# Last head pair's Q and K weights in a third buffer, V_a weights and mask factors issued earlier

## The reference, cut to what matters

```python
h = rms_norm(x, norm_mix_pre)
u_a, v_a, q, k, v_b, g_a, g_b = split(h @ w_in)
# branch A: chunked causal gating
v = layer_norm(gelu(v_a)); y_a = gelu(u_a) * (tril(w_s) @ v + b_s)     # per chunk and group
# branch B: each head under (window, dilation) = (128,1), (512,4), (2048,16)
s = q k^T / 8 - slope * distance;  p = exp(s - max);  o = p v_b / sum(p)  # mixed by the denominators
merged = sigmoid(g_a + b0) * (y_a @ w_a_proj) + sigmoid(g_b + b1) * (y_b @ w_b_proj)
x = x + rms_norm(merged @ w_out)
x = x + rms_norm(square(relu(rms_norm(x) @ w_ff1)) @ w_ff2)
```

## Time and profile before

| | us |
|---|---|
| three runs, median (lowest to highest) | 1197.66 (1196.62 to 1198.12) |
| the profiled execution, its own time | 1197.87 |
| its span on the slowest core (core 5) | 1196.3 |
| PE busy in it | 1112.4 (93%) |
| DVE busy | 742.4 (62%) |
| ACT busy | 529.0 (44%) |
| POOL busy | 133.7 (11%) |

### The profile page before, as it was taken

One profiled execution on the slowest core, in us unless ns is written; L12 is line 12 of the kernel. 1 busy time (PEld: TensorE's weight loads), 2 busy tenths in 40 slices (PEclk: granted clock), 3 DMA queues, 4 the chain that ended last, 5 costly groups with the idle time before them and its releaser, 6 DMA issues.

```text
span 1196.3 us, 20810 instructions; the slowest of 8 cores (1191.0 to 1196.3 us)
## 1 busy us (share of the span) xinstructions
PE 1112.4 (93%) x7304; PEld 564.6 (47%) x7304; DVE 742.4 (62%) x1230; ACT 529.0 (44%) x797; POOL 133.7 (11%) x235
## 2 busy tenths in 40 slices
PE   3799999999878999999999999889999999999994
PEld 1376556655445444544444444434444444444441
DVE  5757777777757643854554556877783167773426
ACT  5537877788846764122122135563321124331120
POOL 0000000001110431000000012530000031000013
PEclk9899999999989999999999999999999999999997
DMA  9558877788713418987677879964466469548413
GB/s 234 141 134 172 148 152 136 153 146 148 116 41 56 72 18 115 115 192 213 176 183 202 224 218 277 300 212 149 154 200 222 142 189 301 177 149 272 145 71 141
DMA packets 94183, 197.55 MB, mean 165 GB/s; under 512 B 39041, under 2 KB 55553, under 8 KB 89218
## 3 DMA queue, kind: packets, MB, share of 16 engines
q1 hardware_dynamic: 83778, 150.08, 41.3%
q0 software_dynamic: 10304, 46.14, 24.2%
HBM read 194.11 MB, written 56.62 MB: 210 GB/s over the span
## 4 chain that ended last, share of the span: by engine, by line
PE 80%; DVE 5%; issue 5%; ACT 4%; DMA 4%; POOL 2%; SPq 0%; DVEq 0%; POOLq 0%; ACTq 0%
PE pst L195 79%; ACT sb_Et L629 2%; DMA sb_xt<-x 1%; DMA sb_gfin<-gains 1%; DMA sb_wva<-w_va 1%; DVE sb_hx L1180 1%; ACT sb_Lr L700 1%; PE pst L199 1%; POOL sb_st L978 1%; DVE sb_sn L1178 1%; POOL sb_st L980 0%; DVE pst L1178 0%; DVE sb_xo L992 0%; ACT sb_junk L1164 0%; DVE sb_hT L497 0%
## 5 line engine op out<-in xcount | busy, mean ns | idle before, releaser
L629 ACT ACTIVATE sb_Et<-pst 128x1024 bf16<-128x1024 f32 (+1 forms) x160 | 150.3, 973 | 43.9 <-PE pst L195 29.7
L195 PE MATMUL pst<-sb_r,sb_hid 128*128 128x512 bf16 x640 | 139.1, 379 | 0.0
L641 DVE TENSOR_TENSOR sb_PT<-sb_Et,sb_EB 128x1024 bf16<-128x1024 bf16 (+2 forms) x200 | 110.2, 569 | 39.2 <-ACT sb_Et L629 25.7
L195 PE MATMUL pst<-sb_hT,sb_wqk 128*128 128x512 bf16 x512 | 126.3, 394 | 0.9 <-DVE sb_hT L497 0.9
L195 PE MATMUL pst<-sb_merged,sb_r 128*128 128x512 bf16 x512 | 121.6, 379 | 1.2 <-DVE sb_tp L990 1.2
L926 ACT ACTIVATE sb_sg<-pst,sb_small 128x512 f32<-128x512 f32 x64 | 44.0, 687 | 172.7 <-PE pst L195 120.0
L195 PE MATMUL pst<-sb_hT,sb_wg 128*128 128x512 bf16 x512 | 116.7, 379 | 0.0
L1074 ACT ACTIVATE sb_sn<-pst 128x512 f32<-128x512 f32 x96 | 57.0, 597 | 106.3 <-PE pst L195 105.9
L195 PEld LDWEIGHTS pst<-sb_r,sb_hid 128*128 128x128 bf16 x640 | 62.6, 98 | 75.6
L195 PE MATMUL pst<-sb_TB,sb_r 128*128 128x512 bf16 x384 | 94.5, 384 | 0.3 <-DVE sb_hid L1077 0.3
L195 PEld LDWEIGHTS pst<-sb_merged,sb_r 128*128 128x128 bf16 x512 | 50.0, 98 | 61.6 <-issue 2.0
(11 more groups left out here) (117 smaller groups left out, 1605.3 us busy)
## 6 DMA issues: line engine op xcount, KB each, us to landing
w_bf<-w POOLq DMA_DIRECT2D x32, 512.0 KB, 10.0
sb_PB<-w_bf SPq DMA_DIRECT2D x32, 512.0 KB, 6.5
w_comb<-sb_PB SPq DMA_DIRECT2D x32, 512.0 KB, 5.4
sb_r<-w_comb SPq DMA_DIRECT2D x32, 512.0 KB, 4.2
sb_r<-w_comb SPq DMA_DIRECT2D x16, 1024.0 KB, 5.0
sb_r<-w_bf SPq DMA_DIRECT2D x32, 384.0 KB, 4.0
sb_r<-w_bf SPq DMA_DIRECT2D x12, 1024.0 KB, 5.0
sb_xt<-x SPq DMA_DIRECT2D x16, 512.0 KB, 12.5
```

Source lines behind the costliest of these rows:

```text
L195: e.matmul(out, lhsT=l, rhs=r, start=st, stop=sp, skip_group_check=True))
L629: P.act(lambda e: e.activation(out=et[:, :, 0:W], in_=psall[:, sb:sb + 2, 0:W], func=AF.Exp, scale=0.125), 2 * W, [], [et.key()], [sb, sb ...
L641: P.dve(lambda e: e.tensor_tensor(out=o, in0=i0, in1=i1, op=ALU.mult), n, rk, [pt.key()], rate=2, name="mask")
```

## The change

Pair 7's Q and K weights get a buffer of their own, `wqk2`, at 64 KiB, over the parts of `stgV0` for classes 0 and 1. Their load is no longer recorded with pair 5 (priority 560) but with pair 6 (570), and depends on pair 5's output passes of classes 0 and 1 instead of on `proj_qk(5)`. The four quarters of `wva` get priorities 620 to 623 instead of 720 to 723. `load_eb(hp + 1)` gets priority `b0 - 10` instead of `b0 + 50`, ahead of `load_v(hp + 1)` at `b0 + 15` or `b0 + 40`. The homes of `hTc` for tiles 0 to 6 become 68, 70, 92, 104, 160, 64, 66.

```diff
@@ -425,6 +425,7 @@
     wqk = [buf(f"wqk{i}", (144 + 4 * i) * K, [8, 256]) for i in range(2)]
+    wqk.append(buf("wqk2", 64 * K, [8, 256]))
     wvb = [buf(f"wvb{i}", (152 + 4 * i) * K, [8, 256]) for i in range(2)]
@@ -459,7 +460,7 @@
     def load_wqk(hp, prio, after=None):
-        d = hp % 2
+        d = hp % 2 if hp < NHP - 1 else 2
         P.dma("pool", lambda e: e.dma_start(out=wqk[d][:].rearrange("p k c -> p (k c)"), in_=wqk_d[hp]), 1e6, f"wqk{d}", [],
@@ -526,8 +527,9 @@
-                P.pe([(ps(bk), wqk[d][:, kc, 128 * j:128 * j + 128], hT[:, kc, 512 * w:512 * w + 512], kc == 0, kc == 7, 512, False)
-                      for kc in range(8)], [wqk[d].key(), hTw[w]], [bk])
+                wq = wqk[d if hp < NHP - 1 else 2]
+                P.pe([(ps(bk), wq[:, kc, 128 * j:128 * j + 128], hT[:, kc, 512 * w:512 * w + 512], kc == 0, kc == 7, 512, False)
+                      for kc in range(8)], [wq.key(), hTw[w]], [bk])
@@ -713,9 +715,11 @@
         if hp < NHP - 1:
-            load_eb(hp + 1, b0 + 50, anchor[0] or gate[15])
-            if hp < NHP - 2:
+            load_eb(hp + 1, b0 - 10, anchor[0] or gate[15])
+            if hp < NHP - 3:
                 load_wqk(hp + 2, b0 + 60)
+            elif hp == NHP - 2:
+                load_wqk(hp + 1, b0 - 30)
@@ -747,14 +751,14 @@
-    hTc = [buf(f"hTc{i}", o * K, [8, 128]) for i, o in enumerate((64, 66, 68, 70, 92, 104, 160, 198, 200, 202))]
+    hTc = [buf(f"hTc{i}", o * K, [8, 128]) for i, o in enumerate((68, 70, 92, 104, 160, 64, 66, 198, 200, 202))]
@@
         P.dma("pool", lambda e, q=q: e.dma_start(out=wva[:, 2 * q:2 * q + 2, :].rearrange("p k c -> p (k c)"), in_=wva_d[q]), 1e6, f"wva{q}",
-              [], [wva.key((2 * q, 2 * q + 2))], prio=M0 - 80 + q)
+              [], [wva.key((2 * q, 2 * q + 2))], prio=M0 - 180 + q)
```

## The result

The changed kernel took 1201.53 us (median of 8 runs, 1198.07 to 1205.31) against 1197.81 for the kernel before (8 runs): a ratio of 1.0032, 95% interval 1.0019 to 1.0045. It is slower, by 3.7 us. The likeliest case had +1.1 us, 1198.8, and its own range, 1196 to 1200, did not hold; the whole range, 1193 to 1203.5, did. Rival two (the load held up behind the V reload, +3.1 with the landing of one bad core) describes what happened.

A forecast was written before the change was run, and what follows sets the result against it. PE, busy 93% of the span, was taken as the bound. Its losses, 18.55 us after against 17.5 before, gave +1.1 us on 1197.87; with the median 0.2 lower, 1198.8 us; own range 1196 to 1200, whole range 1193 to 1203.5.

The forecast's parts named there:

- The likeliest case: Whole kernel: PE loses 18.55 us after against 17.5 before, +1.1 us, 1198.8 us; chance 0.41.
- Rival two: At Q/K group 0, pair 7's load is held up behind the V reload: +3.1 to +6.5 us, 1200.8 to 1204.2; chance 0.25.
- PE's order up to group 0: After pair 5's scores: two S0 jobs, output pass 2, two S0, then Q/K group 0, reached at about 305.5 us.
- The mask factors: At each pair's start, EB going ahead of the V1 reload gains nothing: zero, at most 0.5 us either way.
- Rival one: At Q/K group 0, pair 7's load lands within 7.4 us, in time: -5.8 us, 1191.9 us; chance 0.27.
- idle until PE is at group 0: From pair 5's last scores (298.0) to Q/K group 0 (305.5), PE idles 3.8 us; bounds 1.5 and 4.5.
- wait for pair 7's weights: Before Q/K group 0, PE waits 4.6 us for the late load, with a landing of 12.0 us.
- lower clock: After the wait at Q/K group 0, PE loses 2.25 us at the lower clock; bounds 0 and 3.5.
- scores of pair 6, first class: In pair 6's first classes, no idle time counted, as moved Q/K groups fill PE: 0 us.
- pair 6's end: Between pair 6's output passes 2 and 3, V_a fillers are missing: 2.9 us idle; bounds 0 and 3.9.
- pair 7 and after attention: In pair 7 and at attention's end, PE's loss stays as before: 1.88 + 3.10 = 5.0 us.
- Rival three: After pair 6's output pass 3, the stall moves to V_a tile 2: about 3 us more, 1202 us; chance 0.07.

The follow-up runs named there:

- experiment seven: Kernel before with only the mask factors' priority changed, so that EB goes ahead of the V1 reload on SP; ratio 0.9998.
- five: Changed kernel with only the two w_bf issues of pair 5's classes 0 and 1 moved to pair 6; ratio 0.9972.
- experiment three: Changed kernel with those w_bf issues moved to pair 6 and V_a quarter 0 issued after pair 7's weights have landed; ratio 0.998, 1195.6 us.
- one: Changed kernel with pair 7's Q and K weights back in wqk1, loaded with pair 5; new priorities and hTc order kept; ratio 0.9984.
- two: Kernel before with only the third home wqk2 for pair 7's Q and K weights, its later load and its use; ratio 1.005.
- nine: The changed kernel again, beside the kernel before on one chip, for the spans of all cores; ratio 1.0045.
- four: Kernel before with a second copy of V_a quarter 1 for V_a tiles 0 to 6, instead of a third weights' home; ratio 0.9976, 1195.8 us.
- eight: Kernel before with the second copy of V_a quarter 1 and pair 5's class 0 and 1 w_bf issues moved to pair 6; ratio 0.9951, 1190.5 us.
- six: Changed kernel without the V reload for pair 6, whose output passes use what pair 4 left in the buffers; ratio 0.9978.

## Why the prediction was right or wrong

*What was right.* The places. The V_a wait is gone on every core. The load takes the w_bf's place at 298 (297.87). PE's order up to group 0 came out, and the arrival there to 1 us. The mask factors are worth nothing (experiment seven). Rival one is real and has its price: where the load is in time, as in five, the median core gains 3.8 us of the 5.8 forecast. The rule of the Trainium skill's "DMA: Bandwidth & Descriptors", section "Anatomy of one DMA — SWDGE (gpsimd) path", gives 3.2 us for this transfer, an estimate. No run reached it: the nearest are the 5.0 to 5.2 us on seven cores of experiment three, with nothing ahead in the queue, and in the loaded queue it was 8.4 to 17.7.

*Where the sum failed: its terms, on core 2.* First two windows on core 2 (stretch and its us; busy us and instructions of PE, PEld, DVE, ACT and POOL; PEclk, DMA share, GB/s):

```profile
348.90:364.40 15.50, 10.90 (x150) 7.47 (x148) 10.34 (x17) 11.23 (x15) 3.08 (x3) 0.89 0.00 1
364.40:392.00 27.60, 26.86 (x325) 16.48 (x322) 19.55 (x34) 18.85 (x26) 3.07 (x7) 1.00 0.29 45
```

| us lost by PE | predicted | measured |
|---|---|---|
| idle until PE is at group 0 | 3.8 | 3.5 (1.89 + 0.93 + 0.70) |
| wait for pair 7's weights | 4.6 | 9.3 |
| lower clock | 2.25 | 4.5 |
| scores of pair 6, first class | 0 | 1.2 |
| pair 6's end | 2.9 | 4.6 (15.50 - 10.90) |
| pair 7 and after attention | 5.0 | 0.7 (27.60 - 26.86) |
| sum | 18.55 | 23.8 |

The wait is the step that failed. It used a landing of 12.0 us, halfway between the landings on the two slowest cores of one execution; the worst core of the next had 17.7, as large as the 17.5 that the earlier trace rows showed and that I had kept for the rival. In the two profiled executions of the changed kernel the longest landings are 17.7 and 16.5. The term had to be the longest over eight cores, not one near the middle. The landings of the earlier trace rows were also misread in the argument against rival two: five of the eight were under 10 us, not four.

The lower clock costs twice what I took, since it is met twice more. It is (3.30 + 0.67) - (1.85 + 0.61) = 1.5 on output pass 2, 5.22 - 3.63 = 1.6 on the two groups, and 3.25 - 1.85 = 1.4 on pair 6's last output pass, after a gap of 1.95 and one of 1.04 us:

```profile
355.17 0.61 PE L195 MATMUL pst<-sb_PT,sb_stgV 128*128 128x128 bf16 x8
355.71 0.61 PE L195 MATMUL pst<-sb_QT,sb_KT 64*128 64x256 bf16 x8
358.28 0.40 PE L195 MATMUL pst<-sb_QT,sb_KT 64*128 64x256 bf16 x4 [1.95 <-ACT sb_Et L631]
359.71 0.41 PE L195 MATMUL pst<-sb_QT,sb_KT 64*128 64x256 bf16 x4 [1.04 <-ACT sb_Et L631]
360.31 3.25 PE L195 MATMUL pst<-sb_PT,sb_V 128*128 128x64 bf16 x40 [0.18 <-DVE sb_ybT L707]
```

That is the bridge between output passes 2 and 3 of pair 6, where V_a tiles 1 and 2 had stood. It was rightly placed, and its idle time, 1.95 + 1.04 + 0.18 = 3.2 us, is near the 2.9 forecast. What was missed is the lower clock behind it, and ahead of it 0.95 us for the copy of a V_a result to `raw` and 0.42 for an output pass. Against that, the end of attention is much cheaper than I kept it at. Of the 14 groups of V_a tiles 0 to 6, all ran before the end of attention in the kernel before, and 12 do now. The two left over stand where PE had idled 3.10 us waiting for the next `hTc` copy, and three of the next tiles follow:

```profile
391.50 0.61 PE L195 MATMUL pst<-sb_PT,sb_stgV 128*128 128x128 bf16 x8
391.95 8.80 PE L195 MATMUL pst<-sb_wva,sb_hTc 128*128 128x512 bf16 x40
400.58 1.88 PE L195 MATMUL pst<-sb_wsTf,sb_onesf 128*128 128x512 f32 x4
```

I had taken the matmuls up to 390.1 as the same before and after, all seven tiles among them, so the fillers were a fixed sum used up in pair 7. A filler not used in one gap is used in the next, which a sum by stretches shows only if the leftovers are carried along.

The same three places in the kernel before:

```profile
297.49 0.56 PE L195 MATMUL pst<-sb_QT,sb_KT 64*128 64x256 bf16 x12
...
390.13 7.03 PE L195 MATMUL pst<-sb_wva,sb_hTc 128*128 128x512 bf16 x24 [3.18 <-POOL sb_hTc L781]
396.99 1.88 PE L195 MATMUL pst<-sb_wsTf,sb_onesf 128*128 128x512 f32 x4
```

Its 24 matmuls at 390.13 take 7.03 us, where at 8.80 for 40 they would take 5.3: 1.7 us at the lower clock that I had missed (the granted clock was 0.75 from 390.13 to 397, and 1.00 in the changed kernel from 391.95 to 400.6). So before lost 17.5 + 1.7 = 19.2, and the two sums differ by 4.6 us. From pair 5's last scores to the `sb_wsTf` matmuls, through the same work, it is 396.99 - 297.49 = 99.5 before and 400.58 - 297.25 = 103.3 after: 3.8 us. My sum leaves 0.8 us unexplained. The medians differ by 3.7 us, but these two executions differ by 5.1, so 1.3 us of theirs lie outside this stretch, most of it behind. That the forecast was off by only 2.6 us is in part luck: the sum after was 5.3 us too small and the sum before 1.7, and they were taken from each other. Rival two's +3.1 is luck too: it was worked out with a landing of 14.1, and with the 17.5 that was nearer to the 17.7 of core 2 it gave +6.5.

*Rival three* (tile 2 takes over the stall) has a small part: the 4.6 us at pair 6's end. On the whole that price is given back at the end of attention. From 348.9 us on the changed kernel loses 4.6 + 1.4 + 0.7 = 6.7 us up to the `sb_wsTf` matmuls, and the kernel before, from 335.26 on and not counting the 2.25 us right behind its stall, 1.88 + 3.10 + 1.7 = 6.7.

*What stays open.* Why some cores are hit and others not, and not the same ones: the longest landing is on core 5 in the profile of before, on core 2 after, on core 1 in the repeat. The traces hold a lead that no run tests: how close the last issue of the V reload comes to the w_bf issue after class 0. On core 2 after, the two are 0.7 us apart (SP's timeline, then POOL's), on the other cores 1.4 to 3.5, the V reload first:

```profile
288.46 0.50 SPq L575 DMA_DIRECT2D sb_V<-v_scr  x1
...
289.12 0.52 POOL L585 DMA_DIRECT2D w_bf<-w  x1 [11.36 <-PE pst L195]
```

The same can be read from six profiled executions, 48 cores: before and one (landing of the w_bf after class 1), after, two and nine (pair 7's weights), and four (the copy). On 16 cores the two issues are less than 1 us apart, and 13 of these have a landing of 13 us or more; of the other 32 cores, 2 have one. Whether the order of issues is the cause, or both follow from something else, is not shown. In three and four the distance from the median to the slowest core is larger than before although nobody waits, or hardly, in the profiled execution; only that execution has a trace, and it was among the quicker ones. Moving the w_bf issues goes with a smaller distance (four 6.5, eight 3.5; against before on the same chip, 2.6 and 0.7 more), which speaks for transfers piling up, but where the slow cores of four lost their time was not seen.

## What to carry to other kernels

A buffer with a later release turns a load with slack into one without: before moving a load, write down when its home comes free, what is in flight on all queues then, and how long the consumer can go on without it. Where a load is late by a variable amount, price it at the longest landing over all cores and seen executions, since the slowest core is the metric; a mean or a median core can hide a loss of this kind. And let the thing that is wanted last wait: the second copy of V_a quarter 1 went into the same bytes, at nearly the same time, in the same loaded queue as pair 7's weights, and had 21 us until it was wanted where they had 8.6.

## What the runs showed of the hardware

- With the w_bf issues and the V reload both there, a 512 KB load took 8.4 to 17.7 us (after, two and nine: 24 cores). With either one away it took 6.7 to 8.0, and with no w_bf and nothing else ahead of it in its queue 5.0 to 6.1. No run left both out with the rest unchanged. Over the 5.0 of experiment three, two delays that simply add up would make 8.6 to 10.6 us of it (6.7 + 6.9 - 5.0 to 7.6 + 8.0 - 5.0, an estimate), so the typical landing may be no more than that; the 13.6 to 17.7 on seven of the 24 cores are more.
- PE fell to the lower of its two clock levels while it was doing small jobs: output pass 2 took 3.30 us instead of 1.86 after 3.5 us of idle time in three pieces, with no long stop among them (granted clock 0.50 from 302.12 to 305.2). It took 2.70 to 3.31 us on all 48 cores of the six profiled executions with the third home (after, two, three, five, six, nine). After nearly the same three pieces at pair 6's end (1.95, 1.04 and 0.2 us) in five of them (after, three, five, six, nine) the output pass was slow on 36 of 40 cores (2.57 to 3.31 us) and at full speed on four (1.85), so equal gaps don't always cost the same.
